# New values of a chunked delta rule formed from k S in each chunk, in place of precomputed w and u

## The reference

```python
u = jnp.einsum('bhnij,bhnjd->bhnid', T, v_beta)
w = jnp.einsum('bhnij,bhnjd->bhnid', T, k_beta * jnp.exp(gc)[..., None])
def step(state, inp):
    q_c, k_c, u_c, w_c, g_c, a_c = inp
    v_new = u_c - jnp.einsum('bhcd,bhde->bhce', w_c, state)
    o = (jnp.einsum('bhcd,bhde->bhce', q_c * jnp.exp(g_c)[..., None], state)
         + jnp.einsum('bhij,bhje->bhie', a_c, v_new))
    g_last = g_c[..., -1]
    k_dec = k_c * jnp.exp(g_last[..., None] - g_c)[..., None]
    state = state * jnp.exp(g_last)[..., None, None] + jnp.einsum('bhcd,bhce->bhde', k_dec, v_new)
    return state, o
```

## Time and profile before

| what | value |
|---|---|
| median of 3 runs | 1966.38 us (1966.3 to 1966.85) |
| the profiled execution's own time | 1963.93 us |
| its span, first to last instruction | 1961.8 us |
| TensorE busy | 1947.2 us, 99% |
| VectorE busy | 1219.6 us, 62% |
| ScalarE busy | 877.0 us, 45% |
| GpSimd busy | 14.7 us, 1% |
| mean granted TensorE clock | 0.999 |
| read from HBM, written | 264.72 MB, 43.53 MB |

### The profile page before, as it was taken

The page is one execution under the profiler, slowest core; times in us unless marked ns, Lnnn a source line. Parts: engine busy times, 40 slices in busy tenths (PEclk is TensorE's granted clock), DMA queues, the critical chain, the costliest instruction groups (busy, mean ns, idle before and its releaser), DMA issues. The chain is left out here.

```text
span 1961.8 us, 26313 instructions
## 1 busy us (share of the span) xinstructions
PE 1947.2 (99%) x10250; PEld 1597.4 (81%) x10250; DVE 1219.6 (62%) x1712; ACT 877.0 (45%) x1300; POOL 14.7 (1%) x31
## 2 busy tenths in 40 slices
PE   9999999999999999999999999999999999999998
PEld 7888888888677888888888888888888788888887
DVE  6767566588889745765545456886664456444534
ACT  6444344433777463543323246852654442222222
POOL 0000000000000000000000000010000000000000
PEclk9999999999999999999999999999999999999999
DMA  6899888454333554355555432551143222323231
GB/s 236 295 302 300 289 286 283 164 195 161 129 108 129 179 190 141 118 182 168 159 185 160 154 109 101 207 182 57 55 151 117 86 97 97 103 90 106 87 107 65
DMA packets 90298, 310.56 MB, mean 158 GB/s; under 512 B 10264, under 2 KB 11800, under 8 KB 90176
## 3 DMA queue, kind: packets, MB, share of 16 engines
q1 hardware_dynamic: 89024, 307.50, 46.6%
q10 hardware_dynamic: 1152, 1.38, 0.2%
HBM read 264.72 MB, written 43.53 MB: 157 GB/s over the span
## 5 line engine op out<-in xcount | busy, mean ns | idle before, releaser
L371 PE MATMUL ps<-Hh,whi 128*128 128x512 f32 x1448 | 567.8, 392 | 2.8 <-ACT P L1357 2.1
L375 PE MATMUL ps<-Hh,wlo 128*128 128x512 f32 x1448 | 563.9, 389 | 0.0
L372 PE MATMUL ps<-Hl,whi 128*128 128x512 f32 x1448 | 563.6, 389 | 0.0
L1154 ACT CAST whi<-raw 128x1024 fp32r<-128x1024 f32 (+2 forms) x346 | 349.2, 1013 | 365.0 <-PE ps L375 323.4
L1880 DVE TENSOR_TENSOR wlo<-raw,whi 128x1024 fp32r<-128x1024 f32 (+2 forms) x267 | 312.1, 1174 | 153.0 <-ACT whi L1154 149.2
L371 PEld LDWEIGHTS ps<-Hh,whi 128*128 128x128 f32 x1448 | 271.8, 188 | 66.0 <-issue 4.3
L375 PEld LDWEIGHTS ps<-Hh,wlo 128*128 128x128 f32 x1448 | 271.8, 188 | 57.3
L372 PEld LDWEIGHTS ps<-Hl,whi 128*128 128x128 f32 x1448 | 271.9, 188 | 55.4 <-issue 0.2
L2019 DVE SCALAR_TENSOR_TENSOR cacc<-upad,gains,cacc 128x512 f32<-128x512 f32 x232 | 160.1, 744 | 0.7
L1965 DVE SCALAR_TENSOR_TENSOR x<-ps,x 128x512 f32<-128x512 f32 x79 | 54.6, 691 | 149.6 <-PE ps L375 149.6
L1941 DVE TENSOR_TENSOR scr<-ps,Rt 128x512 f32<-128x512 f32 x92 | 63.2, 687 | 56.1 <-PE ps L375 39.6
(11 more groups left out here) (397 smaller groups left out, 2903.7 us busy)
## 6 DMA issues: line engine op xcount, KB each, us to landing
raw<-in_w SPq DMA_DIRECT2D x392, 512.0 KB, 4.2
low_parts<-lo SPq DMA_DIRECT2D x58, 512.0 KB, 4.3
wlo<-low_parts SPq DMA_DIRECT2D x58, 512.0 KB, 3.4
late_low_parts<-lo SPq DMA_DIRECT2D x21, 512.0 KB, 5.2
wlo<-late_low_parts SPq DMA_DIRECT2D x21, 512.0 KB, 3.4
raw<-in_w SPq DMA_DIRECT2D x16, 384.0 KB, 3.0
raw<-in_w SPq DMA_DIRECT2D x17, 256.0 KB, 2.6
out<-y SPq DMA_DIRECT2D x8, 256.0 KB, 2.1
```

Source lines behind the costliest of these rows:

```text
L371: e.matmul(out, h[:, kk, :], a, start=part != "last" and k + kk == 0, stop=False)
L372: e.matmul(out, h[:, kk, :], c, start=False, stop=False)
L375: ins = e.matmul(out, lo[:, kk, :], a, start=False, stop=done)
L1154: e.copy(whi[i % WS][:, 0:n], raw[i % RAWS][:, 0:n]).then_inc(*act.tick("whi", ("whi", i)))
```

## The change

The new values are written as T (beta v - beta e^g (k S)). The product k S (`kS`) takes the unscaled keys in `qkv`. VectorE adds it, times -beta e^g by partition, to `vb` (`state_taken`, four instructions of 128 columns for a chunk, as in the new state). TensorE multiplies by T (`new_values`, one group of four products), and VectorE copies the result over `vb`. The products for u and w, their copies, and `kbg` are gone. The output's product with the state moves ahead of the row of sums, so that only the product with `aT` is left behind the new values. One first half product of `w_out` stands in each of the chunks 1 to 3, and one more ahead of the last row of sums. VectorE's `on_unit` is split in three (`on_gate`, `on_unit`, `yd_low`); the gate now waits for ScalarE's square too. `kdec`, `Ypl`, `Ydl` and `rows` move to other places in SBUF.

```diff
-            for g in range(4):
+            def new_values(c):
+                b = take(("new", c))
+                if c:
+                    pe.wait_ge("X", c)
+                else:
+                    pe.wait_ge("TT5", 0)
+                for h in range(4):
...
+                    ins = e.matmul(b[:, 128 * h:128 * h + 128], TT[:, h, c, :], vb[:, h, c, :], start=True, stop=True)
+                ins.then_inc(*pe.tick("rule", ("new", c)))
+
+            pool_out(0)
+            new_values(0)
+            for g in range(1, 4):
                 pool_out(g)
             ring.append(bank_of["zg", 3])
...
-            for h in range(4):
-                b, c_ = take(("u", h)), take(("w", h))
...
-                    ins = e.matmul(b[:, 128 * blk:128 * blk + 128], TT[:, h, blk, :], vb[:, h, blk, :], start=True, stop=True)
...
-                    ins = e.matmul(c_[:, 128 * blk:128 * blk + 128], kbg[:, h, blk, :], TT[:, h, blk, :], start=True, stop=True)
...
             for c in range(4):
-                cur, v_ = St[c % 2], vn[c % 2]
-                new = lambda h: u_[:, h, 0, :] if c == 0 else v_[:, h, :]
+                cur, v_ = St[c % 2], vb[:, :, c, :]
+                queries = lambda h: qkv[:, h, 4 + 128 * c:132 + 128 * c]
                 if c:
-                    b = take(("wS", c))
-                    pe.wait_ge("wT", 3)
+                    b = take(("kS", c))
                     pe.wait_ge("St", c)
                     for h in range(4):
-                        ins = e.matmul(b[:, 128 * h:128 * h + 128], wT[:, h, c, :], cur[:, h, :], start=True, stop=True)
-                    ins.then_inc(*pe.tick("rule", ("wS", c)))
+                        ins = e.matmul(b[:, 128 * h:128 * h + 128], qkv[:, 4 + h, 4 + 128 * c:132 + 128 * c], cur[:, h, :], start=True, stop=True)
+                    ins.then_inc(*pe.tick("rule", ("kS", c)))
+                    o = take(("o", c))
+                    for h in range(4):
+                        e.matmul(o[:, 128 * h:128 * h + 128], cur[:, h, :], queries(h), start=h == 0, stop=False)
                     on_row(c - 1)
-                    if c >= 2:
-                        first_half(c - 2)
-                    pe.wait_ge("vn", c)
+                    first_half(c - 1)
+                    new_values(c)
                 else:
-                    pe.wait_ge("u_", 3)
+                    o = take(("o", c))
+                pe.wait_ge("vn", c)
                 if c < 3:
                     b = take(("kv", c))
...
-                        ins = e.matmul(b[:, 128 * h:128 * h + 128], kdec[:, h, c, :], new(h), start=True, stop=True)
+                        ins = e.matmul(b[:, 128 * h:128 * h + 128], kdec[:, h, c, :], v_[:, h, :], start=True, stop=True)
...
-                o = take(("o", c))
                 for h in range(4):
...
-                    if c:
-                        e.matmul(oo, cur[:, h, :], qkv[:, h, 4 + 128 * c:132 + 128 * c], start=True, stop=False)
-                    ins = e.matmul(oo, new(h), aT[:, h, c, :], start=c == 0, stop=True)
+                    ins = e.matmul(o[:, 128 * h:128 * h + 128], v_[:, h, :], aT[:, h, c, :], start=c == 0, stop=c == 0 or h == 3)
                 ins.then_inc(*pe.tick("rule", ("o", c)))
-            first_half(2)
+            first_half(3)
             on_row(3)
-            first_half(3)
             first_half(4)
             first_half(5)
```

ScalarE:

```diff
-            for h in range(4):
-                act.wait_ge("u", h)
-                e.copy(flat(u_, h), ps(("u", h))[:, :]).then_inc(*act.tick("u", ("u_", h), ("free", ("u", h))))
...
             for c in range(4):
-                if c >= 2:
-                    after(("w2", c - 2, "first"))
                 if c:
+                    after(("w2", c - 1, "first"))
                     on_high(c - 1)
                 on_square(c)
                 if c:
                     yd_high(c - 1)
-            after(("w2", 2, "first"))
+            after(("w2", 3, "first"))
             on_high(3)
-            after(("w2", 3, "first"))
+            after(("w2", 4, "first"))
             yd_high(3)
```

VectorE (in `keys` the product for `kbg` is gone; the 16 columns `beg` get a factor of -1):

```diff
+            def on_gate(c):
...
                 dve.wait_ge("o", c)
+                dve.wait_ge("on_sq", c)
                 if c >= 2:
                     dve.wait_ge("ydh", c - 2)
...
+            def state_taken(c):
+                dve.wait_ge("kS", c)
+                dve.wait_ge("beg")
+                for h in range(4):
+                    b = 80 + 4 * c + h
+                    ins = e.scalar_tensor_tensor(out=vb[:, h, c, :], in0=ps(("kS", c))[:, 128 * h:128 * h + 128], scalar=tc[:, b:b + 1], in1=vb[:, h, c, :], op0=MUL, op1=ADD)
+                ins.then_inc(*dve.tick("X", ("X", c), ("free", ("kS", c))))
+
+            def new_values(c):
+                dve.wait_ge("new", c)
+                e.tensor_copy(vb[:, :, c, :], ps(("new", c))[:, :].rearrange("p (h c) -> p h c", h=4)).then_inc(*dve.tick("vn", ("vn", c), ("free", ("new", c))))
...
+            new_values(0)
+            pool_low(0)
+            pool_low(1)
             new_state(0)
-            pool_low(0)
+            pool_low(2)
+            pool_low(3)
+            weights(ends["w2", 0, "first"] + 1)
             for c in range(1, 4):
...
+                state_taken(c)
+                on_gate(c - 1)
+                if c >= 2:
+                    yd_low(c - 2)
+                new_values(c)
                 if c < 3:
                     new_state(c)
...
+                after(("w2", c - 1, "first"))
                 on_unit(c - 1)
-            after(("w2", 2, "first"))
+            yd_low(2)
             after(("w2", 3, "first"))
+            after(("w2", 4, "first"))
+            on_gate(3)
             on_unit(3)
+            yd_low(3)
```

More of the change, by code:

```diff
@@ L224, in build @@
         aT = ph2("aT", [128, 4, 4, 128])
-        rows = ph2("rows", [128, 2, T])
         o_up = off[0]
         up = ph2("up", [128, 4, 528])
+        o_rows = off[0]
+        rows = ph2("rows", [128, 2, T])
         St = [at(f"St{i}", o_up + 2048 * i, [128, 4, 128]) for i in range(2)]
-        vn = [at(f"vn{i}", o_up + 4096 + 2048 * i, [128, 4, 128]) for i in range(2)]
-        u_, wT = vb, Tm
+        assert o_rows + 8192 <= PB + 83584
         turned_g = (scr[5], scr[2])
@@ L242, in build @@
         id32 = c2[:, 288:320].unsqueeze(1).to_broadcast([128, 16, 32])
-        kbg, kdec = at("kbg", PB + 8 * 2064, [128, 4, 4, 128]), at("kdec", PB + 4 * 2064, [128, 4, 4, 128])
-        Yph, Ypl = at("Yph", LOW, [128, 4, T], F32R), at("Ypl", o_TT, [128, 4, T], F32R)
-        Ydh, Ydl = at("Ydh", LOW + 8192, [128, 4, T], F32R), at("Ydl", PB + 8 * 2064, [128, 4, T], F32R)
+        kdec = at("kdec", PB + 8 * 2064, [128, 4, 4, 128])
+        Yph, Ypl = at("Yph", LOW, [128, 4, T], F32R), at("Ypl", o_rows, [128, 4, T], F32R)
+        Ydh, Ydl = at("Ydh", LOW + 8192, [128, 4, T], F32R), at("Ydl", o_Tm, [128, 4, T], F32R)
         off[0] = PB
@@ L822, in tensor_program @@
             i_p, wp_h, wp_l = piece("w_pool_2", 0, 4, [(0, 128)])
-            for g in range(4):
+            def new_values(c):
[5 more added lines that the diff above has]
+                for h in range(4):
+                    if c == 0:
+                        pe.wait_ge("TT6", h // 2)
+                        pe.wait_ge("vb", h)
+                    ins = e.matmul(b[:, 128 * h:128 * h + 128], TT[:, h, c, :], vb[:, h, c, :], start=True, stop=True)
[3 more added lines that the diff above has]
+            for g in range(1, 4):
                 pool_out(g)
             ring.append(bank_of["zg", 3])
-            pe.wait_ge("TT5", 0)
-            for h in range(4):
-                b, c_ = take(("u", h)), take(("w", h))
-                pe.wait_ge("TT6", h // 2)
-                pe.wait_ge("vb", h)
-                for blk in range(4):
-                    ins = e.matmul(b[:, 128 * blk:128 * blk + 128], TT[:, h, blk, :], vb[:, h, blk, :], start=True, stop=True)
-                ins.then_inc(*pe.tick("uw", ("u", h)))
-                pe.wait_ge("kbg", h)
-                for blk in range(4):
-                    ins = e.matmul(c_[:, 128 * blk:128 * blk + 128], kbg[:, h, blk, :], TT[:, h, blk, :], start=True, stop=True)
-                ins.then_inc(*pe.tick("uw", ("w", h)))
             def first_half(j):
@@ L2409, in tcol @@
             def tcol(what, h):
-                a = {"beta": 0, "dec": 64, "beg": 80}[what]
+                a = {"beta": 0, "dec": 64}[what]
                 return tc[:, a:a + 16].rearrange("p (b h) -> p b h", h=4)[:, :, h].unsqueeze(2).to_broadcast([128, 4, 128])
@@ L2497, in keys @@
                 dve.wait_ge("kt", h)
-                dve.wait_ge("beg")
                 dve.wait_ge("vv", 3)
-                e.tensor_tensor(kbg[:, h, :, :], p4(("kt", h)), tcol("beg", h), MUL).then_inc(*dve.tick("kbg", ("kbg", h)))
-                e.tensor_tensor(kdec[:, h, :, :], p4(("kt", h)), tcol("dec", h), MUL).then_inc(*dve.tick("kbg", ("kdec", h), ("free", ("kt", h))))
```

(19 more changed lines are left out.)

2 lines of the change are left out of this document (removed).

## The result

| | before | changed |
|---|---|---|
| median of 6 runs | 1966.62 us (1963.95 to 1969.73) | 1977.31 us (1975.94 to 1980.71) |
| span of the profiled execution | 1961.8 us | 1974.0 us |
| first pool product to first second half product | 42.48 us | 52.68 us |

The changed kernel is slower: ratio 1.0056, 95% interval 1.0046 to 1.0067, 10.7 us by the medians. Of the 12.2 us between the two spans, 10.20 lie in the stage that the prediction walked through. So what stands behind the stage did shift whole.

A forecast was written before the change was run, and what follows sets the result against it. TensorE's queue, busy 99%, was taken as the bound. Waits of 12.45 us, less 0.8 before and 3.58 of removed work, gave +8.1; with 1.7 for the clock +9.8, so 1976.2 us, range 1973.0 to 1979.0.

The forecast's parts named there:

- first state late for kS(1): Chunk 0 to 1: TensorE waits for VectorE's first state, queued behind two pool low parts; 1.75 us.
- turn of the new values: Chunks 1 to 3: nothing on TensorE covers the wait for VectorE's copy before k^T v; 3.1 us in all.
- turn of the state: Between k^T v and the next kS one output group stands instead of two; 0.58 us, twice, 1.2 in all.
- F1 and R2 for their banks: First half product 1 and row of sums 2 wait for VectorE's gates to free output banks; 0.33 and 1.24 us.
- F4 for its bank: First half product after the last row of sums waits for VectorE's last gate to free the last output's bank; 4.8 us.
- clock: After the wait of nearly 5 us TensorE restarts at half clock; 1.7 us, bounds nothing to 4.1.
- Removed work: Delta rule stage: 17 groups of four products on TensorE instead of 21; 3.58 us less.
- the 0.8 of before: TensorE's waits in the same stage of the kernel before, some 0.8 us, subtracted from the new waits.
- The products for kbg cost nothing: Four products of some 0.69 us ahead of the stage, their removal costed at nothing; 2.7 us gain at most.
- the half clock in two places: Kernel's start and end: the trace was said to agree that half clock is the default and activity lifts it.
- under F4 and F5: Second halves' own data come 2.3 us after the last gate, covered by the last two first half products.
- The rival with only the last bank wait gone: Variant of the rival that bank waits don't bind (chance 0.09): only the last one gone, +3.3 us, 1969.7.

The follow-up runs named there:

- experiment 2: Changed kernel with VectorE's last gate ahead of its two weight splits, banks as they were; stage 46.59 us, one run 1971.64 us.
- Experiment 5: Changed kernel, TensorE's list untouched, first state, gates, last root and low part moved earlier on VectorE, last rounded part on ScalarE; stage 42.99 us, one run 1966.83 us.
- experiment 6: Changed kernel with the output's product with the state moved between the new values and the wait for their copy; stage 43.08 us, median 1967.64 us, ratio 0.9997.
- experiment 4: Kernel before, with the first half product after the last row of sums given the last output's bank; stage 44.70 us, one run 1970.18 us.
- experiment 1: Changed kernel, half product after the last row given the last new values' bank; the next one thereby got the last output's; stage 47.99 us, ratio 1.0036.
- Experiment 3: Changed kernel with five unread fp32 products on TensorE between the last row of sums and the next half product; stage 50.64 us, ratio 1.0049.
- experiment 8: Changed kernel with reordered queues and output product moved, half products of chunks 1 and 2 cut, ScalarE's first square earlier; stage 39.49 us, ratio 0.9982.

## Why the prediction was right, step by step

The forecast was 1976.2 us and a shift of 9.8; measured were 1977.31 and 10.7, and 10.20 in the stage itself. All terms below are taken from the timeline after.

| step | predicted, us | measured, us |
|---|---|---|
| first state late for kS(1) | 1.75 | 1.75 (1371.28 + 0.894 to 1373.92) |
| turn of the new values, 3 times | 3.1 | 3 x 0.94 (1379.41 to 1381.25, less 0.894, and so on) |
| turn of the state, twice | 1.2 | 0.58 + 0.49 |
| F1 and R2 for their banks | 0.33 + 1.24 | 0.23 (no bracket; 1385.58 + 0.91 to 1386.72) + 1.15 |
| F4 for its bank | 4.8 | 4.72 (1406.19 + 0.91 to 1411.82) |
| clock | 1.7 | 2.07 (4.82 less 2.75) |
| first group behind a wait | not in the sum | 0.07 to 0.14 longer each, some 0.8 in all |

**Removed work.** TensorE has 10218 records where it had 10250: 32 fewer, four groups of eight. The measured column also closes only with them: 11.7 of waits, 2.07 and 0.8, less 3.58 and the 0.8 of before, is 10.2. The products for kbg cost nothing, as taken: from the products at line 787 to the first pool product both kernels take 13.1 us (1352.3 to 1365.42 before, 1353.6 to 1366.72 after).

**Waits.** The terms were right in place and releaser, and none was too small: 11.7 us against 12.45 in all. Experiments 2, 5 and 6 took terms away and experiment 4 put one into the kernel before, and each stage came out within 0.25 us of its expectation; experiment 1 missed by 0.6, by the slip in the edit.

**The bank of the last output** made two thirds of the loss (4.72 us and 2.07 through the clock, of 10.2). Experiments 1 and 4 are the strongest evidence: whichever half product has that bank starts 5.64 us after the row, in either kernel.

**The clock** was mis-sized by 0.4 us: the term came from the start of the kernel, where 4.55 us of work took 6.29, and F4 was at half clock for longer (4.26 us, against some 3.5 there). The prediction says that the trace shows the half clock in two places. At the end of the kernel it does, by the granted clock. At the start only the pace shows it, two records in a microsecond until 5 us and four after that; the granted clock (the number after POOL) reads 1.00 throughout:

```profile
4.00:5.00 1.00, 1.00 (x2) 0.33 (x1) 0.00 (x0) 0.57 (x1) 0.00 (x0) 1.00 1.04 394
5.00:6.00 1.00, 1.00 (x4) 0.51 (x3) 0.39 (x1) 0.67 (x2) 0.00 (x0) 1.00 1.03 391
```

The Trainium skill, page "TensorE: Matmul & The Clock Gate", section "Terms", reckons the penalty of throttled time as that time times (1 - K/N), where K of every N clock pulses pass, here half. For the 4.26 us that F4 ran so, an estimate by that rule is 2.13 us; the trace shows 2.07, so they agree. Over the whole low stretch, 1409.24 to 1416.08, the same rule would give 3.4, so here it holds for the part in which TensorE worked. Experiment 3 shows cause and effect apart.

**What was luck.** The total came closer than its terms. The waits were 0.7 us smaller than predicted; the clock was 0.4 larger, and the slower first groups, which the prediction did not have, added the 0.8. So 9.8 for 10.20 is in part errors that offset. The last 0.5 us of the measured 10.7 lie outside the stage, and six executions of the kernel before alone reach over 5.8 us.

**What was not right.** The sentence that the second halves' own data come "under F4 and F5" was true only while F4 waited. With that wait gone and the change's queues otherwise kept, TensorE waits for them, 0.6 us in brackets in experiment 2 and 1.5 in experiment 6, because the change put row 3 behind F3. Experiment 5, where the last root and low part also go ahead of a weight split, has no such wait. The rival with only the last bank wait gone was priced at +3.3 and is +4.1 in experiment 2, mostly for that reason. A wait hides the next one behind it; the price of a rival has to be walked to the end as the forecast was.

## What to carry to other kernels

Where each engine has a fixed list, taking products away buys only their own time, while a longer chain through another engine costs its turn, here 1.8 to 2.5 us from the start of one group to the start of the next, of which only 0.9 is TensorE's own work, unless other work stands in it. After a reorder, list which bank each product gets and where in its engine's list the reader that frees it stands: one gate behind two weight splits cost 4.7 us, and 2.1 more through the clock, against 3.6 saved. Then put independent work (the product with the state, a quarter of a half product) under each turn; the same idea so arranged is the fastest of all.

## What the runs showed that I had not expected

The kernels differ from run to run ahead of the stage, in code that none of these edits touches on TensorE. Most of it lies in the 32x32 products of the inverse (line 718), from the first to the last start, here in the kernel before, in experiment 4 and in experiment 8:

```profile
L718 PE MATMUL ps<-scr,scr x1024: 184/191/212, 1318.1 to 1349.9; 32*32 32x32 f32 x171
```

```profile
L718 PE MATMUL ps<-scr,scr x1024: 184/191/214, 1318.4 to 1353.8; 32*32 32x32 f32 x171
```

```profile
L718 PE MATMUL ps<-scr,scr x1024: 184/191/234, 1318.8 to 1354.4; 32*32 32x32 f32 x171
```

That is 31.8, 35.4 and 35.6 us for the same list; the ten profiles lie between these. With the stage taken off, the spans of the ten reach from 1919.3 to 1923.8 us, a range of 4.5. The length of this stretch has a range of 3.8, and its start one of 2.1 (1318.1 to 1320.2). The view of waits puts 0.4 us of it on TensorE's own issue in the kernel before, 2.1 in experiment 4 and 2.5 in experiment 3. What feeds it late was not tried and stays open. It is as large as the effects at stake in experiments 6 to 8, so for such changes the length of the stage in a profile says more than a median of few runs.
